# Expert results: the gate in the eviction, and an adding scatter into the residual rows

## The reference

```
h      = h + mix @ w_out
logits = rmsnorm(h) @ w_router + b_router
gates  = softmax(top4(logits))                       # 4 per token
y_e    = glu(x @ w1[e] + b1[e]) @ w2[e] + b2[e]      # for the tokens of expert e
h      = h + sum over the token's 4 experts of gate_e * y_e
out    = rmsnorm(h) * norm_final_g
```

## Time and profile before

| | us |
|---|---|
| median of 3 runs | 2510.88 (2507.67 to 2510.98) |
| profiled execution, whole | 2508.89 |
| its span | 2507.1 |
| PE busy, share of the span | 2225.3 (89%) |
| DVE busy | 1469.5 (59%) |
| ACT busy | 1104.7 (44%) |
| POOL busy | 275.3 (11%) |
| routing block | about 1208 to 1246.6 |
| expert block | 1246.6 to 2467.2 |
| final block | 2467.2 to 2507.1 |

### The profile page before, as it was taken

How to read it: one execution, slowest core, us unless ns; L and a number is a source line. 1 busy time by engine, 2 the same in 40 slices (tenths; PEclk the granted TensorE clock), 3 DMA queues, 4 the chain that set the end, 5 groups by cost and what they waited for, 6 DMA issues and landing times. The chain is left out here.

```text
span 2507.1 us, 25675 instructions
## 1 busy us (share of the span) xinstructions
PE 2225.3 (89%) x9006; PEld 1435.3 (57%) x9006; DVE 1469.5 (59%) x1309; ACT 1104.7 (44%) x919; POOL 275.3 (11%) x180
## 2 busy tenths in 40 slices
PE   5799979979793799998689999999999999999981
PEld 2455545645543344447466666667667666666651
DVE  2322330463636200001478989988898998899874
ACT  3322221332404100000167777777777777777661
POOL 0000002041423100000010110111011011101100
PEclk8899989989895899999589999999999999999996
DMA  6111012133113422202279999999999999999964
GB/s 178 36 51 51 17 68 84 51 118 105 63 67 101 178 84 84 78 22 95 90 266 358 361 369 360 357 365 357 360 356 364 358 357 368 358 356 357 366 237 179
DMA packets 159811, 528.30 MB, mean 211 GB/s; under 512 B 15414, under 2 KB 81368, under 8 KB 123864
## 3 DMA queue, kind: packets, MB, share of 16 engines
q1 hardware_dynamic: 152376, 505.96, 54.7%
q0 software_dynamic: 7392, 21.77, 2.6%
HBM read 510.77 MB, written 21.10 MB: 212 GB/s over the span
## 5 line engine op out<-in xcount | busy, mean ns | idle before, releaser
L1610 DVE TENSOR_TENSOR w_low<-weights,w_high 128x2048 fp32r<-128x2048 f32 x384 | 873.5, 2288 | 122.4 <-ACT w_high L1604 116.5
L1604 ACT ACTIVATE w_high<-weights 128x2048 fp32r<-128x2048 f32 x384 | 735.4, 1917 | 336.7 <-PE ps L1699 230.3
L1699 PE MATMUL ps<-w_high,rows_high 128*96 128x512 f32 x1024 | 405.4, 396 | 1.1 <-DVE w_low L1610 1.1
L1699 PE MATMUL ps<-w_high,rows_low 128*96 128x512 f32 x1024 | 403.6, 394 | 0.0
L1699 PE MATMUL ps<-w_low,rows_high 128*96 128x512 f32 x1024 | 402.7, 393 | 0.0
L1757 PE MATMUL ps<-w_high,act_high 128*96 128x512 f32 x512 | 206.6, 403 | 29.9 <-DVE w_low L1610 29.9
L1699 PEld LDWEIGHTS ps<-w_high,rows_low 128*96 128x96 f32 x1024 | 165.8, 162 | 71.7
L1699 PEld LDWEIGHTS ps<-w_high,rows_high 128*96 128x96 f32 x1024 | 165.9, 162 | 71.2 <-DVE w_low L1610 2.3
L1699 PEld LDWEIGHTS ps<-w_low,rows_high 128*96 128x96 f32 x1024 | 166.1, 162 | 69.6
L1757 PE MATMUL ps<-w_high,act_low 128*96 128x512 f32 x512 | 201.8, 394 | 0.0
L1757 PE MATMUL ps<-w_low,act_high 128*96 128x512 f32 x512 | 201.1, 393 | 0.0
(11 more groups left out here) (288 smaller groups left out, 2509.4 us busy)
## 6 DMA issues: line engine op xcount, KB each, us to landing
weights<-in_w SPq DMA_DIRECT2D x384, 1024.0 KB, 5.9
weights<-in_w_in SPq DMA_DIRECT2D x32, 1024.0 KB, 5.3
weights<-in_w_in SPq DMA_DIRECT2D x16, 512.0 KB, 5.1
temps<-cum_rows SPq DMA_DIRECT2D x8, 1024.0 KB, 7.1
weights<-cum_rows SPq DMA_DIRECT2D x8, 1024.0 KB, 11.1
weights<-in_w_up_ssd SPq DMA_DIRECT2D x8, 1024.0 KB, 6.2
weights<-expert_rows SPq DMA_DIRECT2D x16, 512.0 KB, 10.2
ssd_out_T<-temps SPq DMA_DIRECT2D x4, 1024.0 KB, 3.9
```

What stands on the lines that cost most here:

```text
L1604: nc.scalar.activation(w_hi[:, split_at(it, j)], slot(at, 1)[:, 0, :], ACT.Copy).then_inc(w_hi_ok, 1)
L1610: nc.vector.tensor_tensor(w_lo[:, split_at(it, j)], slot(at, 1)[:, 0, :], w_hi[:, split_at(it, j)].bitcast(F32), ALU.subtract).then_inc(w_ ...
L1699: last = nc.tensor.matmul(ps[0:CAP, n, :], a[:, k, :], w[:, cols], start=False, stop=k == UP - 1 and i == 2)
```

## The change

Results no longer go to rows of their own. The residual rows `h3` are stored to HBM (`h_d`, `residual_rows`) at the end of the routing block, each expert's result is multiplied by its gate as ACT evicts it, and the scatter adds it into the token's row of `h_d` inside the transfer (`compute_op=ALU.add`). `slot_of` carries four numbers in place of two: the token's row, the same row less 4096 for dropped slots, and the gate in two parts that sum to it. The final block loads 4 tiles in place of 16 and has no multiply-adds; the gain is loaded early, over `h3[:, 0]`, and is multiplied in before the root is known; the last scaling is shared by DVE and ACT.

```diff
@@ routing block
                 for half in range(2):
                     sp.dma_start(b1_rows[half * NE:(half + 1) * NE, :], b1).then_inc(b1_in, 16)
+                for t in range(NT):
+                    sp.wait_ge(h_ok, NT + t + 1)
+                    sp.dma_start(h_d[t * P:(t + 1) * P, :], h3[:, t, :]).then_inc(h_out, 16)
+                sp.wait_ge(h_out, 16 * NT)
+                sp.dma_start(h3[:, 0, :], norm_final_g.rearrange("(a n) -> a n", a=1).broadcast_to([P, D])).then_inc(gf_in, 16)
...
                 then(nc.vector.tensor_scalar(tok_far, tok_id, -FAR, None, ALU.add))
-                then(nc.vector.tensor_copy(tmp_r, tok_far.unsqueeze(2).broadcast_to([P, NT, NE])))
-                for k in range(1, TOPK):
-                    then(nc.vector.scalar_tensor_tensor(tmp_r, one_hot[k], float(k * SEQ), tmp_r, ALU.mult, ALU.add))
-                slots4 = slot_of[:, :].rearrange("p (e t two) -> p t e two", t=NT, two=2)
-                then(nc.vector.tensor_copy(slots4[:, :, :, 1], tmp_r))
+                slots4 = slot_of[:, :].rearrange("p (e t four) -> p t e four", t=NT, four=4)
                 then(nc.vector.tensor_copy(slots4[:, :, :, 0], tok_id.unsqueeze(2).broadcast_to([P, NT, NE])))
+                then(nc.vector.tensor_copy(slots4[:, :, :, 1], tok_far.unsqueeze(2).broadcast_to([P, NT, NE])))
+                then(nc.vector.tensor_copy(slots4[:, :, :, 2], g_dense))
+                then(nc.vector.tensor_tensor(slots4[:, :, :, 3], g_dense, slots4[:, :, :, 2].bitcast(F32), ALU.subtract))
...
-                pe.wait_ge(rt_v, 45)
+                pe.wait_ge(rt_v, 43)
@@ expert block
-                last = nc.tensor.matmul(ps[0:CAP, 6, 400:402], sel[:, t, :], slot_of[:, bass.ds((it % NE) * NT * 2 + t * 2, 2)],
+                last = nc.tensor.matmul(ps[0:CAP, 6, 400:404], sel[:, t, :], slot_of[:, bass.ds((it % NE) * NT * 4 + t * 4, 4)],
...
             nc.vector.tensor_scalar(to_f[0:CAP, bass.ds(it % 4, 1)], ps[0:CAP, 6, 401:402], FAR, None, ALU.add).then_inc(ix_ok, 1)
+            nc.vector.tensor_reduce(gate_f[0:CAP, bass.ds(it % 4, 1)], ps[0:CAP, 6, 402:404], AX.X, ALU.add).then_inc(ix_ok, 1)
...
             nc.vector.tensor_copy(to_i[0:CAP, :], to_f[0:CAP, bass.ds(it % 4, 1)]).then_inc(to_ok, 1)
+            nc.vector.tensor_copy(gate_w[0:CAP, :], gate_f[0:CAP, bass.ds(it % 4, 1)]).then_inc(to_ok, 1)
...
-            pool.indirect_dma_start(out=res_d, out_offset=bass.IndirectOffsetOnAxis(ap=to_i[0:CAP, :], axis=0), in_=ye[0:CAP, :],
-                                    in_offset=None, bounds_check=TOPK * SEQ - 1, oob_is_err=False).then_inc(ye_out, 16)
+            pool.indirect_dma_start(out=h_d, out_offset=bass.IndirectOffsetOnAxis(ap=to_i[0:CAP, :], axis=0), in_=ye[0:CAP, :],
+                                    in_offset=None, bounds_check=SEQ - 1, oob_is_err=False, compute_op=ALU.add).then_inc(ye_out, 16)
...
-            nc.scalar.activation(ye[0:CAP, :].rearrange("p (a b) -> p a b", a=2), ps[0:CAP, 4:6, :], ACT.Copy).then_inc(ye_ok, 1)
+            act.wait_ge(to_ok, it * 2)
+            alone(act)
+            nc.scalar.activation(ye[0:CAP, :].rearrange("p (a b) -> p a b", a=2), ps[0:CAP, 4:6, :], ACT.Copy, scale=gate_w[0:CAP, :]).then_inc(ye_ok, 1)
...
                 end = after_last(pool)
+                before = eng_before(pool)
+                pool.wait_ge(h_out, 16 * NT)
                 for it in range(4):
                     gather_pool(pool, it, it % 2)
@@ final block
+            @block.sync
+            def _(sp):
+                for t in range(NT):
+                    sp.dma_start(fin[:, t, :], h_d[t * P:(t + 1) * P, :]).then_inc(r_in[t], 16)
+                for t in (0, 2):
+                    sp.wait_ge(h_v, NT + 5 + t // 2)
+                    sp.dma_start(out[t * P:(t + 1) * P, :], fin[:, t, :]).then_inc(f_out, 16)
+                for t in (1, 3):
+                    sp.wait_ge(fin_n, t // 2 + 1)
+                    sp.dma_start(out[t * P:(t + 1) * P, :], fin[:, t, :]).then_inc(f_out, 16)
...
+                    nc.scalar.activation(fin_junk, fin[:, t, :], ACT.Square, accum_out=stat[:, t:t + 1]).then_inc(h_sq, 1)
+                act.wait_ge(h_v, NT + 3)
+                nc.scalar.activation(stat[:, 8:12], stat[:, 4:8], ACT.Sqrt).then_inc(h_sq, 1)
+                act.wait_ge(h_v, NT + 4)
+                for t in (1, 3):
+                    act.wait_ge(h_g, t + 1)
+                    nc.scalar.activation(fin[:, t, :], fin[:, t, :], ACT.Copy, scale=stat[:, 12 + t:13 + t]).then_inc(fin_n, 1)
...
             @block.vector
             def _(v):
                 for t in range(NT):
-                    v.wait_ge(r_in[t], 16 + 16 * TOPK)
-                    for k in range(TOPK):
-                        if k:
-                            v.wait_ge(acc_ok, t * TOPK + k)
-                        nc.vector.scalar_tensor_tensor(h3[:, t, :], rows4[:, t, k, :], gate[:, t, k:k + 1], h3[:, t, :],
-                                                       ALU.mult, ALU.add).then_inc(acc_ok, 1)
+                    v.wait_ge(h_sq, NT + 2 + t)
+                    nc.vector.tensor_tensor(fin[:, t, :], fin[:, t, :], nf_bc, ALU.mult).then_inc(h_g, 1)
...
+                v.wait_ge(h_g, NT)
+                for t in (0, 2):
+                    nc.vector.tensor_scalar(fin[:, t, :], fin[:, t, :], stat[:, 12 + t:13 + t], None, ALU.mult).then_inc(h_v, 1)
```

More of the change, by code:

```diff
@@ L79, in build @@
         xn_d = nc.dram_tensor("ffn_rows", (SEQ, D), F32).ap()
-        res_d = nc.dram_tensor("expert_rows", (TOPK * SEQ, D), F32).ap()
+        h_d = nc.dram_tensor("residual_rows", (SEQ, D), F32).ap()
         weights = sb("weights", RING * UNIT)
@@ L1377, in build @@
         b1_lo = sem("b1_lo")
+        h_out = sem("h_out")
         before_experts.close()
@@ L1388, in build @@
         pick = sb_r("pick", CAP)
-        slot_of = sb_r("slot_of", 2 * NE * NT)
+        slot_of = sb_r("slot_of", 4 * NE * NT)
         sel_r = sb_r("sel", NT * CAP)
@@ L1559, in build @@
         ix_i, to_i = take(1).bitcast(I32), take(1).bitcast(I32)
-        to_f = take(4)
+        to_f, gate_f = take(4), take(4)
+        gate_w = take(1)
         xe = [take(D) for _ in range(2)]
@@ L1640, in places_dve @@
                 v.wait_ge(ye_out, it * 16)
-            v.wait_ge(ix_ok, it * 2 + 2)
+            v.wait_ge(ix_ok, it * 3 + 3)
             nc.vector.tensor_copy(to_i[0:CAP, :], to_f[0:CAP, bass.ds(it % 4, 1)]).then_inc(to_ok, 1)
+            nc.vector.tensor_copy(gate_w[0:CAP, :], gate_f[0:CAP, bass.ds(it % 4, 1)]).then_inc(to_ok, 1)
         def gather_pool(pool, it, odd):
-            pool.wait_ge(ix_ok, it * 2 + 1)
+            pool.wait_ge(ix_ok, it * 3 + 1)
             if not (isinstance(it, int) and it < 2):
@@ L1654, in scatter_pool @@
             pool.wait_ge(ye_ok, it + 1)
[L1655 removed]
+            pool.wait_ge(to_ok, it * 2 + 1)
             alone(pool)
[L1657 to L1658 removed]
+            pool.indirect_dma_start(out=h_d, out_offset=bass.IndirectOffsetOnAxis(ap=to_i[0:CAP, :], axis=0), in_=ye[0:CAP, :],
+                                    in_offset=None, bounds_check=SEQ - 1, oob_is_err=False, compute_op=ALU.add).then_inc(ye_out, 16)
         def pick_dve(v, it):
@@ L1670, in rows_pe @@
             pe.wait_ge(xe_in, it * 16 + 16)
-            pe.wait_ge(ix_ok, it * 2 + 4)
+            pe.wait_ge(ix_ok, it * 3 + 6)
             for c in range(NK):
@@ L1845, in _ @@
                         gather_pool(pool, pair + odd + 2, odd)
-                scatter_pool(pool, end - 2)
-                scatter_pool(pool, end - 1)
+                scatter_pool(pool, before)
+                scatter_pool(pool, before + 1)
                 pool.wait_ge(xe_in, end * 16 + 32)
@@ L1854, in _ @@
                 slots_pe(pe, 0)
-                pe.wait_ge(ix_ok, 2)
+                pe.wait_ge(ix_ok, 3)
                 slots_pe(pe, 1)
@@ L1902, in build, with _ @@
         r_in = out_w
-        nf_bc, fin_junk = xe
-        acc_ok = sem("acc_ok")
-        rows4 = weights[:, 0:NT * TOPK * D].rearrange("p (t k d) -> p t k d", t=NT, k=TOPK)
-        with nc.Block() as block:
+        fin_junk = xe[0]
+        nf_bc = h3[:, 0, :]
+        fin_n = sem("fin_n")
+        h_g = sem("h_g")
+        fin = weights[:, 0:NT * D].rearrange("p (t d) -> p t d", t=NT)
+        with nc.Block() as block:
+            @block.sync
[8 more added lines that the diff above has]
+                    sp.dma_start(out[t * P:(t + 1) * P, :], fin[:, t, :]).then_inc(f_out, 16)
+                sp.wait_ge(f_out, 32 * NT)
+            @block.scalar
+            def _(act):
+                for t in range(NT):
+                    act.wait_ge(r_in[t], 32)
+                    if t:
+                        act.wait_ge(h_sq, NT + 1 + t)
+                    nc.scalar.activation(fin_junk, fin[:, t, :], ACT.Square, accum_out=stat[:, t:t + 1]).then_inc(h_sq, 1)
[5 more added lines that the diff above has]
```

(16 more changed lines are left out.)

## The result

The changed kernel takes 2493.14 us (median of 4, 2491.96 to 2493.87), the kernel before 2510.59 beside it: ratio 0.9933, 95% interval 0.9915 to 0.995. That is 17.5 us less where 19.7 were forecast, inside the range of my case (2485 to 2498). The profiled executions differ by 15.0 in their spans, 2507.1 and 2492.1.

A forecast was written before the change was run, and what follows sets the result against it. PE was taken to bound the expert block, DVE and transfers the last 39 us. Terms -21.7 + 2.4 - 0.6 + 0.2 = -19.7 gave 2489.2 us for a run like the profiled one, 2491 median; 8-in-10 range 2485 to 2516.

The forecast's parts named there:

- my case: Whole kernel: the forecast's main outcome, 2485 to 2498 us, chance 0.66.
- Final block: End of the kernel: four loads and no multiply-adds let it end at 2485.4 instead of 2507.1, gain 21.7 us.
- The exposed scatters: Last scatter but one and last scatter: the longer adding scatter is on the path twice, cost 2.4 us, bounds 0 and 5.
- x: Adding scatter when nothing else moves: extra landing time over the plain one's 3.4 us, taken as 1.2, between 0 and 2.5.
- The passes between: Adding scatter in the 30 middle passes: lands after 8.5 us, before PE would stop, cost 0.
- The 10.8: Middle passes: scatter landing in us beyond which PE stops, 9.6 free before DVE's index operation plus 1.2 before PE.
- The late scatter: Rival, middle passes: adding scatter lands after 10.8 us, DVE and PE stop each pass, 2527 to 2578 us; chance 0.24.
- The transfers' load: Expert block: 8.4 MB more read over 1180 us, 7 GB/s on 361; no engine waits for weight loads, cost nothing.
- The small DVE operations: Each pass: two DVE operations on 96 rows push the seventh split by 0.1 us, against 1.2 of room.
- The drain: Rival, behind the last scatter: POOL's drain of 5.46 us grows by up to 2.7, giving 2494, inside the main case.
- Late descriptors: Rival, middle passes: POOL's longer preparation waits for a gap between splits, landing 11.3 us, 2498 to 2506; chance 0.08.
- Routing block: Routing block: four DVE operations go, a cast and subtraction come, gain 0.6 us on the path to PE's bias products.

The follow-up runs named there:

- the two runs: The changed kernel with sixteen loads and no multiply-adds in its final block, 2509.44 us; the changed kernel with four loads and sixteen multiply-adds, 2511.80 us.
- one block: The changed kernel with the final block's work written into the expert block, no barrier, SP waiting for the last scatter itself: 2486.63 us.
- sixteen loads: The changed kernel with each tile of the residual rows loaded four times in the final block and no multiply-adds: 2509.44 us.
- two buffers: The changed kernel with two index and gate buffers in turn, so DVE's index operation no longer waits for the scatter before it: 2488.17 us.
- both edits: The changed kernel with two index and gate buffers in turn and the final block's work in the expert block without a barrier: 2481.72 us.
- the same reordering: DVE's index operation one split earlier in its queue: 2510.21 us in the kernel before (against 2510.00), 2520.09 us in the changed kernel.

## Why the prediction held, and where it was off

*Final block, -21.7 forecast, -20.5 measured.* Right in kind. The last square starts 8.3 us after the first load, not 7.5. The third square waits for its transfer until 2479.90, and the last stands right behind it:

```profile
2479.90 1.06 ACT L1939 ACTIVATE temps<-weights 128x1024 f32<-128x1024 f32 x1 [1.14 <-DMA weights<-residual_rows]
...
2481.14 1.06 ACT L1939 ACTIVATE temps<-weights 128x1024 f32<-128x1024 f32 x1
```

That third load is in 7.1 us after the first issue, where the forecast had 6.1. The longest landing of the four is 7.0 us from its own issue; if it is the last load's, issued 1.3 us after the first, that one is in at 8.3 instead of 7.5. From the first load to the first store are 12.0 instead of 11.2, from there to the end 7.3 instead of 6.9. The forecast didn't ask whether loads or multiply-adds alone were the limit; it took both away, and the two runs show that less would have given 2.3 or 6.2.

*The exposed scatters, +2.4 forecast, +4.5 measured.* The two places were right, the size was not. x is 1.6 to 1.8 us and not 1.2: of 3.4 us without company the add makes 5.0, half a microsecond of it on POOL. The forecast had put that part at nothing in this term, though one of its rivals has POOL preparing more for an add. The transfer's own part, 1.1 without company, is near the 1.2. And there was a second price that the forecast left out. PE's clock falls to half while PE idles in the last pass, and stays there for a time after PE starts again: 3.2 us before (start at 2443.13), 4.3 after (start at 2446.18). In the window from 2446 to 2450 us the clock is 0.96 before and 0.50 after. These rows are first of before, then of after:

```profile
2446.00:2450.00 4.00, 4.00 (x19) 2.73 (x18) 1.90 (x2) 1.92 (x1) 0.00 (x0) 0.96 0.00 0
```

```profile
2446.00:2450.00 4.00, 3.82 (x9) 2.61 (x10) 4.00 (x3) 0.00 (x0) 0.00 (x0) 0.50 0.00 0
```

These matmuls start 0.43 us apart at half clock and 0.23 at full, so 1.1 us more at half cost 0.5 of the 1.0 us between DVE's index operation and the last scatter, an estimate; 0.15 is the second small DVE operation, 0.14 lies behind the start of the last eviction, and 0.2 stays unexplained. The run with a plain scatter, 4.4 us faster, gives the sum of these terms.

How long the clock stays at half does not follow from PE's idle time alone: after 11.2, 11.0 and 11.0 us of it (the changed kernel, one block, sixteen loads) it was 4.3, 4.2 and 4.6, after 9.1 and 9.4 (before, plain) 3.2 and 3.0, but after 6.1 it was 5.9 with two buffers and 2.8 with both edits. What decides is open, and with it more than 1 us of what a change to the last pass brings.

*The passes between, 0 forecast, 0.2 measured.* Right. The landing of 8.7 is next to the 8.5 of the sum. The model behind the threshold, PE's room of 1.2 us behind DVE's wait, held when it was forced: the wait of 2.4 us cost 1.06 a pass. The 10.8 itself was a little high. In the changed kernel the index operation stands 9.4 us behind the scatter's start, the seventh split ends at 1716.86 and ACT is released at 1717.5, so the room is 9.4 + 0.7 = 10.1. The longest landing, 9.2, stays inside it. The late scatter was a real rival, one split away.

*The transfers' load:* nothing, as forecast, though the median load lands 1.3 us later (5.9 and 7.2). *The small DVE operations:* 1.56 us from the index operation to the next split instead of 0.97, so 0.6 and not 0.1, and inside the room all the same. *The drain* did not grow with the add. *Late descriptors* did not occur in the middle, where POOL's instruction is at most 1.49 us. It was close: the scatter of 1703.57 ends at 1705.01, and the next split starts at 1705.26.

*Routing block, -0.6 forecast.* The 0.55 are there at the first gather and gone at the first scatter. The step that failed is "on the path": by the reading above, the path ran through a stretch at half clock whose end did not move with the work. The stores of `h3` were hidden, as forecast: SP issues its last load at 1244.72, and DVE's last operation ends at 1246.7.

The errors have one sign. In the two traces they add up to 4.7 us: 1.2 in the final block, 2.1 at the exposed scatters, 0.7 up to the last scatter but one and 0.8 in the stretch that nothing touched. So the total was not right by errors that cancel. What stays open is the 2.5 us between the difference of the medians (17.5) and that of the two profiled executions (15.0). The stretch that nothing touched is 0.8 apart in them, and the interval of the ratio is 9 us wide.

## What to carry to other kernels

A transfer that reads and writes may be longer for free as long as its waiter stands far enough behind it; before using it, measure from the issuing instruction to the waiter's place, and add the room of the next engine: here 9.6 and 1.2 us before the change, and the same reordering cost nothing before and 27 us after. Where two streams of nearly the same length run side by side, a change that shortens only one gives little. And a wait that is free in the middle of a loop can be exposed in its last pass: two buffers there and the removal of one barrier brought 11.4 us more, for 2481.7 in all.

## What the runs showed of the hardware

An indirect transfer that adds its 4 KB rows to HBM costs 0.50 us more on POOL and lands 1.4 us later among the weight loads, 1.6 later alone (7.3 to 8.7, 3.4 to 5.0). POOL's drain at the end of the expert block takes 5.456 us with a plain scatter and with an adding one alike, and 0.28 at the end of the routing block:

```profile
L1833 POOLq DRAIN  x1: 5456/5456/5456, 2467.1 to 2467.1; - x1
```

With the final block's work in the same block it starts at 2466.0, just as long, and runs beside that work. The adding scatter's instruction on POOL is 1.43 us beside an idle DVE and 3.17 beside a split, and the gather's median went from 2.97 to 1.18 us. In the middle pass its start slipped from 0.11 us behind a split's start (1713.26 and 1713.15) to 0.24 ahead of it (1714.33 and 1714.57), where it takes 1.00:

```profile
L1658 POOL DMA_INDIRECT temps<-ffn_rows,temps x34: 917/1177/3027, 1250.5 to 2412.8; - x34
```

Where it starts behind the first of three splits in a row (the changed kernel with the index operation one split earlier, splits from 1725.81 to 1732.49) it takes 5.04 us, and nothing waits for it:

```profile
1726.05 5.04 POOL L1658 DMA_INDIRECT temps<-ffn_rows,temps  x1 [11.25 <-DVE temps L1642]
```

The Trainium skill, "SBUF — State Buffer", section "SBUF: two separate sides", says that of a GpSimd operation that reads SBUF and a DVE operation with two SBUF inputs the one that starts first gets the shared ports for the whole instruction; these durations agree.
